# The paired-lane RWKV section of a two-block model kernel: other activation functions, other copies, a coarser interleaving

## The reference

```
w, a   = sigmoid(low rank + w0), sigmoid(low rank + a0)
decay  = exp(-0.6065 * w), summed along the tokens of a chunk of 32
kk     = k * kk_gain / norm(k * kk_gain)
state  = state * decay - (state kk) (kk a)^T + v k2^T
y      = r . state, then a group norm over the 64 channels, + bonus, * gate
```

## Time and profile before

| | us |
|---|---|
| three runs | 3844.84, 3836.22, 3881.44 |
| median | 3844.84 |
| profiled execution | 3850.05 |
| its span | 3848.3 |
| PE busy over the span | 3582.3 (93%) |
| DVE busy | 2298.1 (60%) |
| ACT busy | 1787.6 (46%) |
| pair section, first to last `gates` | 1536.4 to 1958.7 |

### The profile page before, as it was taken

One profiled execution on the slowest core, in us unless ns is written; L12 is line 12 of the kernel. 1 busy time (PEld: TensorE's weight loads), 2 busy tenths in 40 slices (PEclk: granted clock), 3 DMA queues, 4 the chain that ended last, 5 costly groups with the idle time before them and its releaser, 6 DMA issues.

```text
span 3848.3 us, 77509 instructions
## 1 busy us (share of the span) xinstructions
PE 3582.3 (93%) x29380; PEld 3488.1 (91%) x29380; DVE 2298.1 (60%) x3344; ACT 1787.6 (46%) x2447; POOL 217.2 (6%) x304
## 2 busy tenths in 40 slices
PE   6976889999999899988889899999997999989998
PEld 6976889999999898877779899999997999989998
DVE  3587566655665644555555666566657657746555
ACT  3322455544444543343433565444454545474443
POOL 1272000000000000000000200000000000000000
PEclk9988999999999999899989999999998999999999
DMA  4533456656665554211114566666664655546775
GB/s 130 157 110 109 131 147 179 172 173 182 179 178 169 157 145 124 61 50 50 50 45 116 150 183 174 183 194 182 173 192 122 170 159 143 154 126 188 196 193 142
DMA packets 1103439, 561.54 MB, mean 146 GB/s; under 512 B 23011, under 2 KB 1101429, under 8 KB 1102981
## 3 DMA queue, kind: packets, MB, share of 16 engines
q1 hardware_dynamic: 1100672, 553.98, 51.2%
q10 hardware_dynamic: 1957, 2.83, 0.2%
q0 software_dynamic: 624, 2.13, 0.2%
HBM read 556.77 MB, written 2.10 MB: 145 GB/s over the span
## 4 chain that ended last, share of the span: by engine, by line
issue 89%; POOLq 6%; PE 3%; DVE 1%; ACTq 0%; POOL 0%; ACT 0%; DVEq 0%; DMA 0%
POOLq L728 2%; POOLq L726 2%; POOLq L508 1%; PE ps L347 1%; PE ps L348 1%; PE ps L349 1%; PE ps L522 1%; ACTq L2299 0%; DVE arena L553 0%; POOLq L724 0%; POOLq L2393 0%; PE ps L2323 0%; DVE ps L549 0%; POOLq L2466 0%; POOLq L2469 0%
## 5 line engine op out<-in xcount | busy, mean ns | idle before, releaser
L315 DVE TENSOR_TENSOR w_lo<-raw,w_hi 128x1024 fp32r<-128x1024 f32 (+1 forms) x1136 | 1333.5, 1185 | 869.5 <-ACT w_hi L309 864.0
L309 ACT ACTIVATE w_hi<-raw 128x1024 fp32r<-128x1024 f32 (+1 forms) x1136 | 1143.9, 1016 | 684.8 <-PE ps L349 424.4
L347 PE MATMUL ps<-x_hi,w_hi 128*128 128x272 f32 (+1 forms) x3712 | 1076.0, 290 | 83.9 <-DVE w_lo L315 47.4
L348 PE MATMUL ps<-x_lo,w_hi 128*128 128x272 f32 (+1 forms) x3712 | 1072.0, 289 | 0.0
L349 PE MATMUL ps<-x_hi,w_lo 128*128 128x272 f32 (+1 forms) x3712 | 1071.3, 289 | 0.0
L347 PEld LDWEIGHTS ps<-x_hi,w_hi 128*128 128x128 f32 x3712 | 715.4, 193 | 91.0 <-DVE w_lo L315 51.7
L348 PEld LDWEIGHTS ps<-x_lo,w_hi 128*128 128x128 f32 x3712 | 715.7, 193 | 0.0
L349 PEld LDWEIGHTS ps<-x_hi,w_lo 128*128 128x128 f32 x3712 | 715.3, 193 | 0.0
L431 PE MATMUL ps<-x_hi,w_hi 128*128 128x256 f32 (+1 forms) x1872 | 532.3, 284 | 32.1 <-ACT arena L1785 11.4
L432 PE MATMUL ps<-x_lo,w_hi 128*128 128x256 f32 (+1 forms) x1872 | 526.0, 281 | 0.0
L433 PE MATMUL ps<-x_hi,w_lo 128*128 128x256 f32 (+1 forms) x1872 | 525.9, 281 | 0.0
(11 more groups left out here) (492 smaller groups left out, 4603.7 us busy)
## 6 DMA issues: line engine op xcount, KB each, us to landing
raw<-ffn_w_up SPq DMA_DIRECT2D x352, 512.0 KB, 4.7
raw<-w_in SPq DMA_DIRECT2D x232, 512.0 KB, 3.8
raw<-cd_w_in SPq DMA_DIRECT2D x100, 512.0 KB, 3.8
raw<-ffn_w_down SPq DMA_DIRECT2D x128, 384.0 KB, 3.4
raw<-ab_w_in SPq DMA_DIRECT2D x80, 512.0 KB, 4.0
raw<-ffn_w_down SPq DMA_DIRECT2D x128, 320.0 KB, 3.3
raw<-w_out SPq DMA_DIRECT2D x48, 512.0 KB, 4.0
raw<-ab_w_out SPq DMA_DIRECT2D x32, 512.0 KB, 4.0
```

The source lines that it names most:

```text
L309: nc.scalar.activation(w_hi[:, j % SLOTS, 0:kt], raw[:, j % RING, 0:kt], ACT.Copy).then_inc(rounded, 1)
L315: nc.vector.tensor_tensor(w_lo[:, j % SLOTS, 0:kt], raw[:, j % RING, 0:kt], w_hi[:, j % SLOTS, 0:kt].bitcast(F32), ALU.subtract).then_inc( ...
L347: nc.tensor.matmul(acc, w_hi[:, j % SLOTS, k, 0:w], mh, start=first, stop=False)
L348: nc.tensor.matmul(acc, w_hi[:, j % SLOTS, k, 0:w], ml, start=False, stop=False)
```

## The change

- `rates`: two Sigmoid instructions become two Tanh of half the argument (with new bias vectors `half_w0`, `half_a0`) and two Copy instructions with scale and bias 0.5.
- The Ln of the norm and the Ln of the group norm get positions next to each other, and so do the two Exp behind them.
- The states' additions (`added`) are copied out of PSUM by DVE (three copies per pair, `L1187` and `L1189` in the changed file, and one for the meta tile, L1122), no more by ACT; the stage `add` on ACT goes.
- In the meta tile, the transposes of `ar` and `bend` go to bank Y and p2's products to bank X; those of `kend` and `v` move behind p20. With this PE no longer waits for `tok0` before p20.
- `stream_tensor` gets a `grain`: products are issued in groups of four k tiles.
- All steps of both tables get other numbers.
- A DVE drain is added in `ready`; two small DVE instructions in the setup make the half biases.

```diff
-    def stream_tensor(pe, name, operand):
+    def stream_tensor(pe, name, operand, grain=1):
...
-            k_to = int((pos - v_to) * p.parts[v_to][2]) if v_to < len(p.parts) else 0
+            k_to = int((pos - v_to) * p.parts[v_to][2] / grain) * grain if v_to < len(p.parts) else 0
...
-    EDGE_AT, EDGE_END = timed((("keys", 1.0), ("gates", 1.9), ("rates", 2.0), ("norm", 0.6), ("cum", 3.4), ("decays", 0.1), ("bonus", 2.5), ("ready", 2.9),
+    EDGE_AT, EDGE_END = timed((("keys", 1.0), ("gates", 1.6), ("rates", 2.1), ("norm", 0.6), ("cum", 2.7), ("ln", 1.8), ("exp", 1.7), ("bonus", 0.1), ("decays", 2.0),
...
             scalar("decays")
+            dve.drain()
...
-            yield at("fe0_") + 0.05
-            scalar("add0")
+            yield at("fe0_")
+            tensor("fe0")
+            nc.vector.tensor_copy(L.state0[q % 2], ps[:, X, 2 * P + RW_N:3 * P])
...
-                yield at(f"fe_{tt}") + 0.1
-                scalar(f"add{tt}")
+                yield at(f"fe_{tt}")
+                tensor(f"fe{tt}")
                 first = 4 * (tt - 1)
+                nc.vector.tensor_copy(L.state[:, first + 1:first + 4], ps[:, B:B + 3, 2 * P + RW_N:3 * P])
+                if tt == 1:
+                    nc.vector.tensor_copy(L.state[:, 4], ps[:, B + 1, 3 * P + RW_N:4 * P])
...
-            nc.scalar.activation(L.prev, ps[:, X, 0:T], ACT.Sigmoid, bias=col("cd_rw_w0", p))
-            done(nc.scalar.activation(L.a, ps[:, Y, 0:T], ACT.Sigmoid, bias=col("cd_rw_a0", p)))
-            yield at("norm") + 0.1
+            nc.scalar.activation(L.prev, ps[:, X, 0:T], ACT.Tanh, bias=half_w0[:, p:p + 1], scale=0.5)
+            nc.scalar.activation(L.a, ps[:, Y, 0:T], ACT.Tanh, bias=half_a0[:, p:p + 1], scale=0.5)
+            act.drain()
+            nc.scalar.activation(L.prev, L.prev, ACT.Copy, scale=0.5, bias=0.5)
+            done(nc.scalar.activation(L.a, L.a, ACT.Copy, scale=0.5, bias=0.5))
+            yield at("ln")
             vector("norm")
             nc.scalar.activation(L.x, L.x, ACT.Ln)
             act.drain()
+            yield at("exp")
             done(nc.scalar.activation(L.x, L.x, ACT.Exp, scale=-0.5))
...
-            for b, first, src in ((X, P, L.ar[:, 0]), (X, 2 * P, L.bend), (Y, P, L.kend), (Y, 2 * P, L.v)):
+            for b, first, src in ((Y, P, L.ar[:, 0]), (Y, 2 * P, L.bend)):
...
             vector("q10")
-            scalar("tok0")
-            heads_times(Y, 0, L.q1, of(L.p1), n, n)
-            done(heads_times(Y, 2 * n, L.p1, of(L.q1), n, n))
+            heads_times(X, 0, L.q1, of(L.p1), n, n)
+            done(heads_times(X, 2 * n, L.p1, of(L.q1), n, n))
             yield at("p40")
             vector("y0")
             scalar("p20")
+            for first, src in ((P, L.kend), (2 * P, L.v)):
+                nc.tensor.transpose(ps[0:n, X, first:first + P], src[:, 0:n], ident[:])
...
-        upto = stream_tensor(pe, "mid", operand)
+        upto = stream_tensor(pe, "mid", operand, 4)
```

More of the change, by code:

```diff
@@ L210, in build @@
     ommu, _ = place("ommu", [P, 26])
+    half_w0, _ = place("half_w0", [P, CW])
+    half_a0, _ = place("half_a0", [P, CW])
     dskip, _ = place("dskip", [P, CW])
@@ L1004, in build @@
     EDGE_V = order("keys", "norm", "cum", "bonus", "ready", "q10", "y0", "q40", "y40", "y80", "fe0")
-    EDGE_S = order("rates", "norm", "decays", "tok0", "p20", "p40", "p80", "gin0", "gh0", "add0")
+    EDGE_S = order("rates", "norm", "decays", "tok0", "p20", "p40", "p80", "gin0", "gh0")
     EDGE_T = order("gates", "bonus", "x0", "p20", "p40", "p80", "y80", "gh0", "fe0")
     BODY_V = order(*body_stages("p1", "q1", "y", "q4", "y4", "y8", "z1", "t32", "fe"), "s6", "s7", "s8", "y", "centred", "end")
-    BODY_S = order(*body_stages("tok", "p2", "p4", "p8", "gin", "t16", "gh", "add"), "squared", "log", "rstd")
+    BODY_S = order(*body_stages("tok", "p2", "p4", "p8", "gin", "t16", "gh"), "squared", "log", "rstd")
     BODY_T = order(*body_stages("x", "p2", "p4", "p8", "y8", "z1", "w", "gh", "fe"), "s6", "s7", "s8", "out", "sums", "squares", "gate")
@@ L1019, in timed @@
         return at, now
-    EDGE_AT, EDGE_END = timed((("keys", 1.0), ("gates", 1.9), ("rates", 2.0), ("norm", 0.6), ("cum", 3.4), ("decays", 0.1), ("bonus", 2.5), ("ready", 2.9),
-                               ("x0", 1.3), ("m0", 1.1), ("p20", 0.3), ("p20_", 0.6), ("p40", 0.8), ("p40_", 0.7), ("p80", 0.5), ("p80_", 0.6),
-                               ("y80", 0.2), ("y80_", 0.5), ("gh0", 0.4), ("gh0_", 0.6), ("fe0", 0.5), ("fe0_", 1.2)))
+    EDGE_AT, EDGE_END = timed((("keys", 1.0), ("gates", 1.6), ("rates", 2.1), ("norm", 0.6), ("cum", 2.7), ("ln", 1.8), ("exp", 1.7), ("bonus", 0.1), ("decays", 2.0),
+                               ("ready", 3.3), ("x0", 1.3), ("m0", 1.1), ("p20", 0.4), ("p20_", 1.2), ("p40", 1.0), ("p40_", 1.0), ("p80", 0.6), ("p80_", 0.7),
+                               ("y80", 0.3), ("y80_", 0.6), ("gh0", 0.5), ("gh0_", 0.6), ("fe0", 0.6), ("fe0_", 0.9)))
     BODY_AT, BODY_END = {}, EDGE_END
@@ L1026, in build @@
             ("x", 1.6), ("m", 1.5), ("p2", 1.0), ("p2_", 0.9), ("p4", 1.9), ("p4_", 1.1), ("p8", 1.3), ("p8_", 0.7), ("y8", 0.5), ("y8_", 0.7),
[L1027 removed]
+            ("z1", 0.8), ("z1_", 0.7), ("w", 0.5), ("t32", 0.7), ("gh", 0.5), ("gh_", 0.6), ("fe", 2.6), ("fe_", 2.5))], BODY_END)
         BODY_AT.update(some)
[L1029 to L1030 removed]
+    some, TAIL_END = timed((("s6", 0.5), ("s6_", 0.5), ("s7", 0.5), ("s7_", 0.5), ("s8", 0.5), ("s8_", 0.5), ("out", 1.8), ("y", 0.6), ("sums", 0.5), ("centred", 0.6),
+                            ("squared", 0.7), ("squares", 1.35), ("log", 1.0), ("gate", 4.55), ("rstd", 3.3), ("end", 2.2)), BODY_END)
     BODY_AT.update(some)
@@ L1263, in edge_scalar @@
             done(nc.scalar.activation(L.gin[0:n], ps[0:n, Y, 0:2 * P].rearrange("p (a b) -> p a b", a=2), ACT.Copy, scale=-1.0))
-            yield at("fe0_")
-            tensor("fe0")
-            done(nc.scalar.activation(L.state0[q % 2], ps[:, X, 2 * P + RW_N:3 * P], ACT.Copy))
     def body_scalar(act, lane_n):
@@ L1297, in body_scalar @@
                 done(nc.scalar.activation(L.gin, two_of(B + 2, 0, n), ACT.Copy, scale=-1.0))
-                yield at(f"fe_{tt}")
-                tensor(f"fe{tt}")
-                first = 4 * tt - 3
-                mm = nc.scalar.activation(L.state[:, first:first + 3], ps[:, B:B + 3, 2 * P + RW_N:3 * P], ACT.Copy)
-                if tt == 1:
-                    mm = nc.scalar.activation(L.state[:, 4], ps[:, B + 1, 3 * P + RW_N:4 * P], ACT.Copy)
-                done(mm)
             yield at("squared")
@@ L1311, in body_scalar @@
             act.drain()
+            yield at("rstd") - 0.02
             done(nc.scalar.activation(L.x_end, L.x_end, ACT.Exp, scale=-0.5))
@@ L2348, in start_vector @@
         nc.vector.tensor_scalar(ommu[:], cols("cd_rw_mu", 26), -1.0, 1.0, ALU.mult, ALU.add)
+        for half, name in ((half_w0, "cd_rw_w0"), (half_a0, "cd_rw_a0")):
+            nc.vector.tensor_scalar(half[:], cols(name, CW), 0.5, None, ALU.mult)
         dve.wait_ge(a_exp, 1)
```

13 lines of the change are left out of this document (5 added, 8 removed).

## The result

The changed kernel takes 3930.06 us (median of four runs, 3910.49 to 3932.21), the one before, measured with it, 3840.53. The ratio is 1.0209, with a 95% interval of 1.0164 to 1.0254: slower by 80 us by the ratio and by 89.5 in the medians. I forecast slower by 31 us and a range up to 3910. The direction and the places were right, the size was not.

A forecast was written before the change was run, and what follows sets the result against it. TensorE bounds the kernel, idle 7.6 us per pair. Waits of 14.2 us are 6.6 more, less 2.1 for mode changes: 4.5 us times seven periods, 31 us, so 3876 us; range 3826 to 3910.

The forecast's parts named there:

- Table loads: ScalarE: nineteen fewer loads of 1.283 us, some 3 us per pair; the wait at L1544 moves to VectorE, winning nothing.
- meta bank: Meta tile: p20's 2.1 us wait for L1250 goes, about 0.45 us comes ahead of p40; gain about 1.6 us per pair.
- copies: State copies moved to VectorE: 0.2 to 0.34 us each, costing it 1.1 us per pair, relieving ScalarE of as much.
- Chains A: Start of a pair, from an odd part's last product through `keys` to `gates`: TensorE waits about 2.1 us.
- B: Bonus sum L1347, behind the odd part's end and the state additions on VectorE: TensorE waits about 4.3 us.
- C: Squares' sum, from y8 through VectorE to z1's copy: 2.3 us wait at w and 0.4 us at L1544.
- the adjacent stages: Stages left without products between, such as p4 behind p2: small waits of 0.45 to 1.3 us, 5.1 us together per pair.
- the chains are covered: Rival: added waits overlap, 3.0 us more per pair less 2.1, so 3851 us, no change; chance 0.20.
- Groups of four: Products issued in fours: 15 fewer changes of mode at 0.14 us save 2.1 us per pair, bounds 1.5 and 6.
- The clock: TensorE's granted clock held unchanged in the sum; rival that it falls further: up to 4 us per pair, 3904 us, chance 0.12.
- The period before: Distance between starts of `gates` before the change, taken as 60.3 us, to become some 65 us.
- Seven periods, nothing at the edges: Eight pairs give seven periods of 4.5 us more each, 31 us; the edges outside add nothing.

The follow-up runs named there:

- the repair: Whole change, with VectorE's two instructions for the bonus sum moved 0.2 parts earlier, ahead of the split and the states: 3885.91 us, ratio 1.0138 to the kernel before.
- the last step: Kernel with only tanh, VectorE state copies and other meta bank, plus the norm's Exp moved behind the Square: 3817.95 us, ratio 0.9930 to the kernel before.

## Why the forecast was wrong

*The bound* was read rightly: TensorE, in order, with waits as the loss.

*Table loads, meta bank, copies.* 1.283 us a load, three fewer per pair: right, and the wait that they relieved came back at w, as forecast. The meta bank's gain of about 1.6 us per pair came as 1.8 in the change (2.2 to 0.4, now at L1373). The copies took 0.36 and 0.21 us.

*Chains A, B, C and the adjacent stages* were forecast at 2.1, 4.3, 2.7 and 5.1 us, together 14.2, and measured at 2.1, 4.1, 2.0 and 4.7; the idle time of a period is 12.9 us. What was too large is mainly chain C, by 0.7: w waits 2.0 us and not 2.3, and L1544 does not wait a second time. (The six terms of chain C add up to 6.2 us, not 6.1.) The rival "the chains are covered" is refuted.

*Groups of four* were to save 2.1 us per pair. No run shows it: at the old positions the busy time is 56.1 with single products and 55.4 with groups, and the clock of the second is higher by 0.01 (0.945 against 0.934), which alone is worth 0.6 to 0.7 us. Between the kernel before and the change 0.4 us is left when the cost of the clock is taken out. So the term is at most 0.4 us per pair. It was mis-sized, and so was the growth of the waits: 6.6 us forecast, 4.6 measured, 1.3 of it because the waits with the change were put too high and 0.8 because the idle time before is 8.4 us per period and not the 7.6 of my stretches of 61 us. That the sum of the two, 6.6 less 2.1, came to 4.5 and so close to the measured 4.6 less 0.4 is luck.

*The clock* is the step that failed. The sum held it as it was, and gave more only in a rival: "If a wait of 4.3 us brings one more slow stretch per pair, as long as the 8 us per pair now, up to 4 us more", with a chance of 0.12. The runs show in its place 7.2 us per period, since the time at the lower level went from 6.1 to 20.5 us of it, and with this the forecast period of 64.8 us (or 68.3 from the true 63.77) became 75.1. Products for nothing in the waits took 6.7 us of it back. I also tied the fall to the single long wait. That wait does have a slow stretch of its own, but in the kernel with the gates and w filled it stands with a clock of 0.95; the waits of 2.1, 2.0 and 1.2 us had one each as well, and those I had not counted. The bound of "as long as the 8 us per pair now" had no reason.

*The period before* was taken from seven intervals as 60.3 us, with the short first one in it. It is 63.8 in the steady state. This did not enter the difference, apart from the 0.8 us of idle time named above.

*Seven periods, nothing at the edges.* The first two intervals grew by 5.3 and 5.8 us and not by 11.3, and 14.2 us came behind the last gates, which I had put at nothing. The two nearly cancel: seven times 11.3 is 79 us, and the whole span grew by 82.2. This, too, is luck.

What stays open is by what rule the waits' places set the clock. The runs show that it is not the longest wait alone and not the sum of waits, and that 1.6 us more work per pair, with no wait closed, changes it; a forecast from the old trace would have had to give a wide range for it. Untested are each of the new parts by itself and the added drain of VectorE. Why three profiles start the section some 20 us later was not looked into.

## What to carry to other kernels

In a section whose engine is idle a little in many places, price the clock as its own term and with a wide bound: here more than half of what the change, its repair and the last step cost or won was clock (7.2 us for 3.2 us of idle time in the repair). Count cover at the grain at which it is issued: positions that are harmless with single products and groups that are harmless at old positions lost 2% together. An engine's relief is worth something only where its instruction is the last to arrive, and the wait may come back at the next stage: with one Exp moved behind the Square, L1544 waited 1.6 us less and all of the idle time fell by 0.7. When a forecast comes true, look whether the term that it rested on did.

## What was not expected of the hardware

Work for nothing in waiting time made the program some 30 us faster: 16 products of 128x256 per pair took the clock from 0.86 to 0.95 and the period from 75.1 to 68.4 us. A program can fall into a pattern that repeats to 0.01 us with the clock low at the same stages each time (75.10 us at 0.86), and leave it by 1.6 us of additional work per pair (71.9 us). The same wait of 2.1 us at the gates is followed by a clock of 1.00 in one period and of 0.50 in a later one.
